# Sample attention by chunk over four samples, and three rearranged stage borders, in a hybrid decoder step

## What is computed

```python
mods = split(silu(c) @ w_ada + b_ada, 6)              # conditioning
h = rmsnorm(x, ln1) * (1 + mods[1]) + mods[0]
xr, yr, q, kvc, kvs, kvw, g = split(h @ w_in)         # recurrent input, its gate, queries, three K/V kinds, gates
o_r = scan(conv(xr)) * gelu(yr)                       # RG-LRU recurrence
q_rot, kvs, kvw = rope(q), rope(kvs), rope(kvw)
ckv = gelu((blocks of 64 raw K/V rows + pe) @ w1) @ w2   # compressed branch; for samples over 2048 paged rows
o_c, imp = softmax(q . ckv)                           # importance of each block of 64
idx = the 16 blocks with the highest importance       # first, current and previous one forced
o_s = softmax(q_rot . keys of those blocks) @ values  # samples: keys gathered by page_table
o_w = softmax(q_rot . last 512 keys) @ values
x = x + mods[2] * (concat(rmsnorm(o_r), rmsnorm(g0*o_c + g1*o_s + g2*o_w)) @ w_out)
y = x + mods[5] * swiglu(rmsnorm(x, ln2) * (1 + mods[4]) + mods[3])
```

## Time and profile before

| what | before |
|---|---|
| time, median of 3 runs | 1895.55 us (1894.96 to 1902.36) |
| profiled execution | 1894.68 us, span 1892.9 us |
| instructions | 30414 |
| PE busy | 1722.1 us (91%) |
| DVE busy | 945.7 us (50%) |
| ACT busy | 748.5 us (40%) |
| POOL busy | 292.9 us (15%) |
| mean granted clock of PE | 0.937 of full speed |
| feed-forward and output part | from 987.8 us to the end |

### The profile page before, as it was taken

One profiled execution on the slowest core, in us unless ns is written; L12 is line 12 of the kernel. 1 busy time (PEld: TensorE's weight loads), 2 busy tenths in 40 slices (PEclk: granted clock), 3 DMA queues, 4 the chain that ended last, 5 costly groups with the idle time before them and its releaser, 6 DMA issues. The chain is left out here.

```text
span 1892.9 us, 30414 instructions
## 1 busy us (share of the span) xinstructions
PE 1722.1 (91%) x11011; PEld 1548.5 (82%) x11011; DVE 945.7 (50%) x1770; ACT 748.5 (40%) x1183; POOL 292.9 (15%) x270
## 2 busy tenths in 40 slices
PE   5999959769969898998679979999999999999998
PEld 3988935358858797876449979999999999999997
DVE  3657654324557666664555724444345443444433
ACT  3435401124436465553333435532235432345322
POOL 1100132411000000000006412103305014100032
PEclk8999979978979898998889989999999999999999
DMA  8455220154400000013435464544554544545453
GB/s 285 116 159 167 68 74 1 58 178 150 142 5 2 1 0 1 1 50 156 191 126 135 133 196 118 141 123 122 160 136 123 162 120 137 155 134 137 134 143 93
DMA packets 297093, 214.48 MB, mean 113 GB/s; under 512 B 20317, under 2 KB 284301, under 8 KB 293742
## 3 DMA queue, kind: packets, MB, share of 16 engines
q1 hardware_dynamic: 290348, 172.61, 32.0%
q0 software_dynamic: 4816, 40.73, 5.6%
q10 hardware_dynamic: 1842, 0.05, 0.1%
HBM read 206.07 MB, written 11.41 MB: 115 GB/s over the span
## 5 line engine op out<-in xcount | busy, mean ns | idle before, releaser
L422 DVE TENSOR_TENSOR ff_lo<-ff_raw,ff_hi 128x2048 fp32r<-128x2048 f32 (+1 forms) x126 | 263.6, 2092 | 222.5 <-ACT ff_hi L418 222.5
L427 PE MATMUL banks<-low_rows,ff_hi 128*128 128x352 f32 x1120 | 360.1, 322 | 0.0
L426 PE MATMUL banks<-ff_h_hi,ff_hi 128*128 128x352 f32 x1056 | 342.6, 324 | 13.3 <-DVE ff_lo L422 13.2
L428 PE MATMUL banks<-ff_h_hi,ff_lo 128*128 128x352 f32 x1056 | 340.2, 322 | 0.0
L418 ACT ACTIVATE ff_hi<-ff_raw 128x2048 fp32r<-128x2048 f32 (+1 forms) x126 | 215.4, 1710 | 235.8 <-PE banks L428 220.0
L427 PEld LDWEIGHTS banks<-low_rows,ff_hi 128*128 128x128 f32 x1120 | 211.3, 189 | 0.3
L426 PEld LDWEIGHTS banks<-ff_h_hi,ff_hi 128*128 128x128 f32 x1056 | 199.0, 188 | 14.6 <-issue 14.4
L428 PEld LDWEIGHTS banks<-ff_h_hi,ff_lo 128*128 128x128 f32 x1056 | 199.4, 189 | 0.0
L426 PE MATMUL banks<-hid_hi,ff_hi 128*128 128x352 f32 x528 | 171.9, 325 | 4.3 <-DVE hid_lo L422 4.1
L428 PE MATMUL banks<-hid_hi,ff_lo 128*128 128x352 f32 x528 | 171.0, 324 | 0.0
L427 PE MATMUL banks<-hid_lo,ff_hi 128*128 128x352 f32 x528 | 170.3, 323 | 0.0
(11 more groups left out here) (408 smaller groups left out, 3154.7 us busy)
## 6 DMA issues: line engine op xcount, KB each, us to landing
ff_raw<-in_w_gate SPq DMA_DIRECT2D x66, 512.0 KB, 4.0
ff_raw<-in_w_up SPq DMA_DIRECT2D x66, 512.0 KB, 5.3
ff_raw<-in_w_down SPq DMA_DIRECT2D x48, 384.0 KB, 4.1
late_ada<-in_w_ada SPq DMA_DIRECT2D x16, 1024.0 KB, 5.6
ff_raw<-in_w_down SPq DMA_DIRECT2D x48, 320.0 KB, 3.4
ff_raw<-in_w_out SPq DMA_DIRECT2D x24, 512.0 KB, 5.3
s_raw<-in_w_in SPq DMA_DIRECT2D x48, 128.0 KB, 2.5
streams<-in_x_prompt SPq DMA_DIRECT2D x4, 1024.0 KB, 9.3
```

Source lines behind the costliest of these rows:

```text
L422: return dve.tensor_tensor(lo, raw, hi.bitcast(F32), ALU.subtract)
L426: pe.matmul(out, lhsT=w_hi, rhs=x_hi, start=first, stop=False)
L427: pe.matmul(out, lhsT=w_hi, rhs=x_lo, start=False, stop=False)
L428: return pe.matmul(out, lhsT=w_lo, rhs=x_hi, start=False, stop=last)
```

## The change

Projection: chunks 0 to 3 are rebuilt first (0 and 1 by POOL, 2 and 3 by DVE), then chunks 4 to 7 by DVE in three pieces of 352 columns; ACT takes the last bank. The buffer of `h_lo` becomes the buffer of `w_nat`, so SP loads its first four chunks as soon as chunks 0 to 3 are rebuilt, the other four after the rest, and then stores the last states. `rot` is loaded near the end of the projection.

Keys: the first two pieces of `w1` load after the queries are rotated. The sums of the gate's norm go out after tiles 3, 4 and 6. The laying out of the samples' queries goes to POOL in `prompt_attention`.

Compression: the first gather is issued ahead of the two memsets of POOL; the first prompt rows load without a wait for weights.

Sample attention: the past units go chunk by chunk over the four samples; four units are turned, then four scored, with no turn ahead. DVE takes a chunk after its later copies.

```diff
 project_and_recur, SP
+            sp.wait_ge(ada_summed, ADA + 1)
+            sp.dma_start(rot, d["rot"]).then_inc(rot_loaded, 16)
+            sp.wait_ge(rebuilt_p, 2)
+            sp.wait_ge(rebuilt_v, 2)
+            for c in range(KB):
+                sp.dma_start(w_nat[:, c, 0:NAT_COLS], d["w_in"][0, c * P:(c + 1) * P, NAT_COL:NAT_COL + NAT_COLS]).then_inc(w_loaded[0], 16)
+            sp.wait_ge(rebuilt_v, 2 + NGR)
+            for c in range(KB, KD):
+                sp.dma_start(w_nat[:, c, 0:NAT_COLS], ...).then_inc(w_loaded[1], 16)
             sp.wait_ge(last_copied, 1)
 ACT
+                if n == n_blocks - 1:
+                    act.wait_ge(used, n_blocks)
+                    for j, (a, b) in enumerate(groups):
+                        act.activation(streams[:, n // 2, a:b], ps[NGR * (n // 2 % 2) + j][:, 0:GR], ACT.Copy).then_inc(last_taken, 1)
+                    act.wait_ge(last_taken, NGR)
 POOL
-            for c, after_block in ((0, n_blocks - 1), (1, n_blocks - 1), (KB, n_blocks)):
-                pool.wait_ge(used, after_block)
-                pool.tensor_tensor(hT[:, c, :], ...).then_inc(rows_rebuilt, 1)
+            pool.wait_ge(used, n_blocks - 1)
+            for c in range(2):
+                pool.tensor_tensor(hT[:, c, :], ...).then_inc(rebuilt_p, 1)
 DVE
-            for c in range(2, KB):
-                rebuild(c, n_blocks - 1)
-            take(n_blocks - 1)
-            for c in range(KB + 1, KD):
-                rebuild(c, n_blocks)
+            dve.wait_ge(used, n_blocks - 1)
+            for c in range(2, KB):
+                dve.tensor_tensor(hT[:, c, :], ...).then_inc(rebuilt_v, 1)
+            for j, (a, b) in enumerate(groups):
+                if j < NGR - 1:
+                    dve.wait_ge(rows_free, j + 1)
+                else:
+                    dve.wait_ge(used, n_blocks)
+                dve.tensor_tensor(hT[:, KB:, a:b], h_hi[:, KB:, a:b].bitcast(F32), h_lo[:, KB:, a:b].bitcast(F32), ALU.add).then_inc(rebuilt_v, 1)
 keys_and_values
-        Z_AFTER = {3: 0, 5: 1, 7: 2}
+        Z_AFTER = {3: 0, 4: 1, 6: 2}
-            sp.dma_start(rot[:, :], d["rot"]).then_inc(rot_loaded, 16)
-            for c in range(0, KD, 2):
-                sp.dma_start(w[:, c:c + 2, :], ...).then_inc(w_loaded, 16)
-            sp.dma_start(rope...)
+            sp.dma_start(rope...)
+            sp.wait_ge(queries_rotated, 1)
+            load_w1(sp, d, 0, w1[0], w1_loaded[0])
+            load_w1(sp, d, L_CHUNK // 2, w1[1], w1_loaded[1])
                     for c in range(KD):
+                        if t == 0 and h == 0 and c == KD // 2:
+                            pe.wait_ge(w_loaded[1], 16 * (KD // 2))
-                if t + 1 == len(ROTATED):
+                if t + 2 == len(ROTATED):
                     s.fence()
-                    spread()
+                    dve.sem_inc(queries_rotated, 1)
 compress
-            with sp.Fori(0, TRIPS) as i:
+            prompt(0, 0)
+            prompt(0, 1)
+            with sp.Fori(0, TRIPS - 1) as i:
                 for p in range(2):
-                    sp.wait_ge(multiplied, i * (2 * STEPS) + (p - 1) * STEPS + AHEAD)
+                    sp.wait_ge(multiplied, i * (2 * STEPS) + (p + 1) * STEPS + AHEAD)
+                    load_w1(sp, d, i * (2 * LP) + (2 + p) * LP, w1[p], w1_loaded[p])
+                    prompt(i + 1, p)
-            pool.memset(zero[:, :], 0.0).then_inc(zero_set, 1)
-            pool.memset(w2k[:, :, :], 0.0).then_inc(w2_clear, 1)
                 for g in range(SG):
+                    if n == 0 and g == 1:
+                        pool.memset(zero[:, :], 0.0).then_inc(zero_set, 1)
+                        pool.memset(w2k[:, :, :], 0.0).then_inc(w2_clear, 1)
                     pool.indirect_dma_start(rows[g][p], ...)
 prompt_attention, POOL (and SP waits for queries_spread ahead of load_window)
             pool.memset(vx, 0.0).then_inc(v_clear, 1)
+            s = Steps(pool, queries_spread)
+            s.done(pool.memset(q_plain[:, :, :], 0.0))
+            s.then(pool.memset(q_rot[:, :, :], 0.0))
+            for b in range(BT):
+                for h in range(N_KV):
+                    for dst, src in ((q_plain, qT), (q_rot, qR)):
+                        for g in range(SG):
+                            s.done(pool.tensor_copy(dst[...], src[...]))
 sample_attention
-            return 1 + v % (2 * (CH - 1)) // 2, v // (2 * (CH - 1)) * 2 + v % 2
+            return 1 + v // BT, v % BT
-                def units(a, b, at_once):
-                    for w in range(a, a + at_once):
-                        turn_k(w)
-                    for w in range(a, b, at_once):
-                        if w + at_once < b:
-                            for x in range(at_once):
-                                turn_k(w + at_once + x)
-                        for x in range(at_once):
-                            score(w + x)
+                def units(a, b):
+                    for w in range(a, b, BT):
+                        for x in range(w, w + BT):
+                            turn_k(x)
+                        for x in range(w, w + BT):
+                            score(x)
-                    dve.wait_ge(k_used, g * UN + (BT if c == 0 else UN - 2 * (CH - 1) + 2 * c))
+                    dve.wait_ge(k_used, g * UN + BT * (c + 1))
-                for w in copies:
-                    copy_k(dve, dve.tensor_copy, k_copied_v, g, w)
-                for c in range(1, CH):
-                    take_chunk(c)
+                for n, w in enumerate(copies):
+                    copy_k(dve, dve.tensor_copy, k_copied_v, g, w)
+                    if n:
+                        take_chunk(n)
+                take_chunk(CH - 2)
+                take_chunk(CH - 1)
```

More of the change, by code:

```diff
@@ L98 @@
 N_VEC = _at
+KB_ROWS = KD // 2 * P
 class Steps:
@@ L847, in keys_and_values @@
     with ExitStack() as st:
-        w = sb(nc, st, "w_nat", [P, KD, NAT_COLS])
+        pad = sb(nc, st, "kv_pad", [P, KB_ROWS])
+        sb(nc, st, "kv_weights", [P, KD, ROWS])
         cos_t, sin_t = kT[:, 0, :], kT[:, 1, :]
[L851 to L857, removed]
-        Z_AFTER = {3: 0, 5: 1, 7: 2}
+        spare = 2 * T9 * HALF
+        rope = w[:, 0, NAT_COLS:NAT_COLS + spare].rearrange("p (a t n) -> p a t n", a=2, t=T9)
+        tmp = [w[:, 1 + j, NAT_COLS:NAT_COLS + spare] for j in range(4)]
+        z_sum = [pad[:, 0:GR], sb(nc, st, "z_sum1", [P, GR])[:, :]]
+        Z_AFTER = {3: 0, 4: 1, 6: 2}
         STEPS = KA * NG
@@ L897, in rotate @@
                     c, g = step // NG, step % NG
[L898 removed]
+                    pe.matmul(ps[4 + step % 4][:, 0:GR], lhsT=rot, rhs=qT[:, c, g * GR:(g + 1) * GR], start=True,
                               stop=True).then_inc(rot_summed, 1)
@@ L921, in _ @@
                         pe.wait_ge(z_rooted, g)
-                    pe.matmul(ps[7][:, 0:GR], lhsT=ones[:, :], rhs=z_sum[g % 2][:, :], start=True, stop=True).then_inc(z_summed, 1)
+                    pe.matmul(ps[7][:, 0:GR], lhsT=ones[:, :], rhs=z_sum[g % 2], start=True, stop=True).then_inc(z_summed, 1)
             pe.wait_ge(z_rooted, NG)
@@ L1003, in rotate @@
                     s.done(dve.tensor_tensor(qR[:, c, cols], qR[:, c, cols], qtmp[:, step % 2, :], ALU.add))
-            def spread():
-                s.done(dve.memset(q_plain[:, :, :], 0.0))
-                s.then(dve.memset(q_rot[:, :, :], 0.0))
-                for b in range(BT):
-                    for h in range(N_KV):
-                        part = slice(h * HEAD_DIM, (h + 1) * HEAD_DIM)
-                        c0 = b * QR + h * DEC_SEQ * GROUP
-                        for dst, src in ((q_plain, qT), (q_rot, qR)):
-                            for g in range(SG):
-                                row = SEQ + (g * BT + b) * DEC_SEQ
-                                s.done(dve.tensor_copy(
-                                    dst[part, g * BT + b, c0:c0 + DEC_SEQ * GROUP].rearrange("p (s g) -> p s g", g=GROUP),
-                                    src[part, :, row:row + DEC_SEQ].rearrange("p g s -> p s g")))
-            T = [tmp[:, j, :].rearrange("p (t h n) -> p t h n", h=N_KV, n=HALF) for j in range(4)]
+            T = [tmp[j].rearrange("p (t h n) -> p t h n", h=N_KV, n=HALF) for j in range(4)]
             def rotate_keys(a, b):
@@ L1375, in _ @@
             pool.memset(vx, 0.0).then_inc(v_clear, 1)
+            s = Steps(pool, queries_spread)
+            s.done(pool.memset(q_plain[:, :, :], 0.0))
+            s.then(pool.memset(q_rot[:, :, :], 0.0))
+            for b in range(BT):
+                for h in range(N_KV):
+                    part = slice(h * HEAD_DIM, (h + 1) * HEAD_DIM)
+                    c0 = b * QR + h * DEC_SEQ * GROUP
+                    for dst, src in ((q_plain, qT), (q_rot, qR)):
+                        for g in range(SG):
+                            row = SEQ + (g * BT + b) * DEC_SEQ
+                            s.done(pool.tensor_copy(
```

(3 more changed lines are left out.)

104 lines of the change are left out of this document (56 added, 48 removed).

## The result

The changed kernel takes 1886.05 us (median of 6 runs, 1883.68 to 1889.69); the kernel before, on the same chip, 1896.39 us (6 runs). The ratio is 0.9945, 95% interval 0.9926 to 0.9964: about 10 us less, of which the interval leaves 7 to 14.

The account below looks back on a forecast made before the run. PE was taken as busy for most of the span, its second half PE-bound and fixed, so only PE's idle places could move; the terms summed to -7.8 from 1894.68 us, 1886.9, forecast as 1887, range 1878 to 1897.

Parts of the forecast that it names:

- Projection to keys, -8.7: First border: key product starts at 252.1 instead of 260.84, with `rot` and the first weights already there: -8.7 us.
- Norm of the gate, +4.0: Key product, after tile 4: PE waits 2.6 us for ACT's root and the clock falls, 1.6 more; taken as +4.0.
- The end of the block, -3.3: End of the keys' block: tail keys rotated earlier, so SP's last stores end the block sooner: -3.3 us.
- Compression, -10.3: Second border: weights loaded early and gather issued sooner, so the turns start at 386.0 instead of 396.29: -10.3 us.
- The clock term, -1.6: Compression: zero products keep PE busy until the turns, so the clock does not fall: -1.6 us (ends 0 and -2).
- Queries spread, +3.4: Start of prompt attention: some 14 DVE steps each wait for one 0.24 us POOL copy: +3.4 us.
- the upper end: Start of prompt attention: the POOL copies' cost if DVE and POOL share the port, +9 us.
- sharing: Start of prompt attention: DVE slowed by a factor of 1.9 beside POOL over 10 us of DVE path: +9 us.
- taking turns: Start of prompt attention: DVE and POOL lock the port per instruction, so DVE steps wait for single copies: +3.4 us.
- Sample attention, +8.0 and +2.3: Sample attention: more rounds wait for the fourth sample, each round of four taking 4.2: group 0 +8.0, group 1 +2.3 us.
- The rival that packing pays: Sample attention: four scores cost about as much as two, rounds take 3.25, total 1881 us; chance 0.08.
- The slow rounds: Sample attention: clock stays low, rounds of 6.4, +16, total 1903 us; chance 0.12 together with a larger collision.

Follow-up runs that it names:

- run c: Changed kernel with the eight key-weight loads put back to the head of the keys' block: 1887.76 us, ratio 0.9963.
- run i: Changed kernel with the projection's four last stores issued by ACT instead of by SP behind eight loads: 1885.47 us, ratio 0.9946.
- run b: Changed kernel with the gate norm's second sum moved between the two halves of tile 5: 1882.17 us, ratio 0.9927.
- e: Changed kernel with the earlier kernel's sample attention and the gate norm's second sum between the halves of tile 5: 1871.56 us, ratio 0.9873.
- run d: Changed kernel with the first two pieces of compression weights loaded at the head of the compression again: 1899.45 us, ratio 1.0018.
- run f: Kernel before the change with only the new sample attention added: 1906.34 us against 1894.69, ratio 1.0062.
- run g: Changed kernel keeping its chunk-by-chunk order, but turned and scored by pairs with the next pair turned ahead: 1886.69 us, ratio 0.9960.
- run a: Changed kernel with the sample attention of the kernel before, all else as changed: 1874.32 us, ratio 0.9887.
- h: Changed kernel with the samples' queries laid out twice on POOL at the start of prompt attention: 1886.65 us, ratio 0.9961.

## Why the prediction was right, and where it was not

1887 was forecast and 1886.05 measured, by the mechanisms named: both borders give, the norm's sum and the sample attention take back. That it came out within 1 us is luck: five terms came out slower than forecast by 4.3 us together and three faster by 6.5, so that the stages gave -10.1 for a forecast of -7.8, and in the profiled execution the two stages that scatter took 1.4 of it back.

- *Projection to keys, -8.7:* -7.6. The block started within 0.3 of the forecast, but the rotations ran wholly at a granted clock of 0.50 (windows 252 to 257) and delayed the product by 4.82, not 4.0. What fell short is the cause given, that the weights come early. By run c only 1.3 of the 7.6 hang on that: the early loads are worth 3.6 (run c against run i), but the stores queued behind them cost 1.5 to 2.4 of it. What is left in run c, 6.4, goes with the matrix `rot` being there, the shorter rebuild and the wait for half of the weights; no run parts these three.
- *Norm of the gate, +4.0:* +4.4, cause shown by run b. The end of the block, -3.3: as forecast in sum, though the stores that wait for the tail keys begin 3.9 sooner behind the last tile (3.30 instead of 7.17) and SP's issues take 0.6 longer, which was not counted.
- *Compression, -10.3:* -8.9. The memset came 1.1 behind the gather (1.4 counted), but the gather itself started 0.77 into the block, and the zero products ran wholly at 0.50 (windows 377 to 383; 5.28 to the first turn against 4.4; 4.2 to 4.3 in runs b, e and i). Why the gather starts late is open; in the profiles of all ten kernels that begin with it the delay is 0.77 to 0.79. That the weights were the wait is shown by run d. The clock term, -1.6, was -3.8 from the first turn to DVE's start on the next stage. It is no fixed price: the stretch from the first turn to the first product of prompt attention took 160.61 in the trace of before, 158.04 in run f, where nothing there is changed either, and 156.6 to 159.0 in the others. So no run shows that the change caused the -3.8, and the clock as its cause is not shown either.
- *Queries spread, +3.4:* +0.2, the term that was furthest off. I let every DVE step wait for a copy. The copies are 0.17 each, so DVE loses little to one; the long waits are POOL's., on which the upper end rested, showed DVE beside one long POOL instruction (L673, 3.21, from 236.22 to 239.43), not beside short ones. The mean of 2.26 also hides two different rebuilds (the five rebuilds in the trace of before; shortest, median and longest in ns, first and last start):

```profile
L824 DVE TENSOR_TENSOR hT<-h_hi,h_lo x5: 1243/1246/3347, 237.2 to 245.3; 128x1056 f32<-128x1056 f32 x5
```

The first took 3.35, to 240.55, that is until POOL was done and its own 1.2 behind that; the second took 1.24. So these rows did decide between sharing and taking turns, against what the prediction says: with the factor of 1.9 that was read as sharing, the first would have been over near 239.5.

The Trainium skill (SBUF — State Buffer, "SBUF: two separate sides") has the shared ports locked for a whole instruction by whoever starts first. The trace agrees: each pair of copies lasts about one DVE step (2.31 and 2.43 beside 2.35), and a lock held for 0.17 costs DVE 0.09 in two steps. With 0.17 for each of the 14 steps the term would have been 2.4, with the measured 0.045 a step 0.6; PE's start came 0.2 later.
- *Sample attention, +8.0 and +2.3:* +6.9 and +3.5, in sum 10.4 for 10.3, which hides two errors. In group 0 the fourth sample's turn came 25.59 after the start of the stage, not the 26.90 of before (25.80 and 25.74 in runs f and g, 27.14 in run a, so it goes with the order; why is not shown). In group 1 the clock fell behind the wait, which the prediction did not count. Rounds are 4.4 instead of 4.2: the third turn waits 0.40, and four scores take 1.80 to 1.98. Runs a and f show that the changed stage costs this and nothing else does; run g, that nearly all of it is the order: the wait for the fourth sample, with the slow stretch behind it.

The rival that packing pays is refuted: from two to four scores the time goes from 1.05 to 1.80, 0.19 for each added instruction. The prediction's "about 1.1 at full" for four scores was read off a stretch at half speed and halved; the trace of before had four scores at a granted clock of 1.00, at 966.84, and they took 1.91. The Trainium skill (TensorE: Matmul & The Clock Gate, "Part 3: Packing small matmuls — row/col tiling") has packed products end within a few ns of one; these scores of float32 do not, and the measurement decides. The slow rounds did not come either: in both groups turns are back at 1.09 by the second pair behind the fourth sample's.

## What to carry to other kernels

Count what stands behind the last arrival: an order that is even over the data makes nearly all of the work wait for the last piece, one that uses up the early pieces leaves only the work of the last pieces behind it, and here that was worth 10 to 12 us, as much as the whole change gained. When a load is moved ahead, look at what is now queued behind it and at how much of it the consumer needs to begin: the early loads were worth 3.6 us, and the stores behind them took up to 2.4 of it; the product began 7.7 us after the first load where it needed half of them (run c) and 11.5 where it needed all (before), a difference between two kernels that no run parts from the rest. Compare from event to event: most stage lengths repeat to a few tenths, while runs of one kernel lie 2 to 9 us apart.

## Hardware behaviour that was not expected

- The wait of 2.61 us after tile 4 stands alike in seven profiles. In five of them (the change, a, d, g, h) the granted clock falls behind it, the two tiles take 22.68 to 22.80 and the sum 1.21 to 1.33; in c and i it stays at 1.00, and they take 21.44 and 0.83. A clock cost read from one trace is a possible price, not a sure one.
- A short POOL copy beside long DVE steps is stretched sevenfold (0.35 to 2.31 a pair), with DVE slowed by 0.09 in 4.60. It goes the other way too: a DVE copy that takes 0.17 took 0.95 when POOL had begun a memset of 0.95 ahead of it (532.73 in the trace after).
